# The keys of a three-layer transformer kernel projected once instead of twice, with 28 dense chunks spread over 32 scan units

## The chip, the cores and the metric

The kernel runs on one core of a Trainium2 chip as a single program. The metric is the device time of one execution in microseconds; shown is the median of the runs. The profile comes from one further execution.

## The reference

The input is `x` of 512 tokens by 1024 features, in float32. It passes through two layers of a first block, and through one layer of a second block.

```
for l in range(2):                                  # first block
    h = rms_norm(x); proj = h @ w_in[l]             # sb_q, sb_k, sb_v, sw_q (8 heads), sw_k, sw_v (2 heads), gates
    y_sb  = stick_breaking_attention(sb_q, sb_k, sb_v) @ w_branch_sb
    q, k  = rope(rms_norm per head(sw_q)), rope(rms_norm per head(sw_k))   # heads of 64
    y_swa = sliding_window_sink_attention(q, k, sw_v) @ w_branch_swa
    x = x + (sigmoid(gates) * (y_sb, y_swa) summed) @ w_out
    x = x + square(relu(rms_norm(x) @ w_up)) @ w_down
h = rms_norm(x) * (1 + scale) + shift               # second block
z, xbc, dt, q, kc, vc, ks, vs, kw, vw, gates... = h @ w_in_2     # q: 16 heads; each key and value: 2 heads of 64
y_ssm = mamba2(z, conv(xbc), dt)                    # chunked scan: 4 chunks of 128 tokens, 32 heads
y_nsa = attention over compressed, selected and windowed keys kc, ks, kw (rotated) and values vc, vs, vw
x = x + gate * (merged @ w_o); x = x + gate2 * mixture_of_experts(x); out = rms_norm(x)
```

Eight query heads share two key heads in the sliding window attention (four each), and sixteen share two in the second block. So a key head has 64 rows, and 128 rows hold both.

## The kernel before, in words

**Layout.** Activations lie feature-major: 128 partitions hold 128 features, 512 columns are the tokens. A key head of 64 features fills one half of the partitions. A matmul of a query head with a key head wants both in the same half. The even query heads are in the lower half, the odd ones in the upper half, so each of the two key heads is wanted in both halves. The kernel gets this by projecting each key head twice: `twice` loads the 64 weight columns of a head into two places of the weight tile, so that one chunk of 128 output rows holds the same head in both halves.

**Weight tiles.** Weights come in tiles of 1024 rows by 256 columns (1 MB). SyncE issues four loads into `raw[q]` (`W.issue`, L169), as soon as that place's last tile has been split. ScalarE writes a rounded part `hi` (`split_hi`, L176, 1.9 us), VectorE the rest `lo` (`split_lo`, L181, 2.3 us). A place `q` of 0 or 1 is split again when the tile in it is done. A tile gives two chunks (`dense(2t)` and `dense(2t+1)`) of 128 output rows. A chunk is 8 k-steps of three matmuls of 128 x 512 (`products`, L199 to L201): 24 matmuls.

**`mix` (first block, once per layer).** TensorE, ScalarE, VectorE and SyncE each run a queue written out by hand. Tiles 0 to 17 are: 0 the keys, 1 and 2 the window's queries, 3 the window's values, 4 and 5 values, 6 to 9 queries and keys, 10 to 17 gates. Chunks of tiles 0 to 7 alternate between PSUM banks 0 and 1; from tile 8 on (`ONE_BANK`) all are written to bank 0, so each waits for the eviction (L855) of the one before. The keys need: the two chunks of tile 0, `square` of each, `head_sums` (L562) of each, the mean, root and reciprocal (`mean_of`, `root_of`, `scale_by`) of each, and a rotation (`rotate`, L583, and `rope`, L887 to L893) of each. The queries need `query_sums` (L568), `query_mean` and four rotations. Rotations follow chunks 10 to 15, the keys' last. Then `band_scores(0)` (L593) starts the window's attention.

The first eviction needs the token factor `x_rs`, whose mean, root and reciprocal are made on VectorE and ScalarE at the beginning of `mix`.

**The scan (`ssd`, second block).** The state-space scan runs in 32 units (8 groups of 4 heads, 4 chunks of tokens). TensorE's queue is, for each unit n: `front(n+1)`, in odd units a `step` (L1665 to L1667), `dense(n+2)`, `back(n)` (L1696, L1698, L1702). The dense chunks are the projections of z (16 chunks), q (8) and the keys and values of the second block (8: kc, vc, ks and kw, two chunks each, by `twice`). ScalarE and VectorE follow with `exps` and `segment`, `weigh`, `finish`. `back(n)` waits for `weigh(n)`. Each chunk is evicted by ScalarE (L1734) into a stage of four, from where GpSimd's queue sends it to HBM (`spilled`, 128 rows by 512). Behind every second chunk the next tile but one is split.

```
for n in range(N):
    if n + 1 < N:
        front(n + 1)
    if n in due:
        step(due[n])
    if n + 2 < N:
        dense(n + 2)
    back(n)
```

**Behind the scan.** `ssm_out` loads six key chunks back (L1940) and eight query chunks (L1942) from HBM, rotates the keys late in the stage (L1969), and issues the weights of the next gates behind these loads on SyncE's queue. `nsa_project` loads the two value chunks `vc`.

Of the kernel before, what the change touches and what calls it, by code (L numbers as in the profile page):

```python
# [344 lines left out]
class FirstBlock(Kernel):  # L345
# [5 lines left out]
    def layer_tile(self, l, m, q):  # L351
# [4 lines left out]
        if t == T_SWK:  # L356
            return self.twice(w_in, C_SWK)
# [20 lines left out]

    def twice(self, w, at):

        out = []
        for j in range(2):
            src = w[:, at + j * HD:at + (j + 1) * HD].rearrange("(k p) n -> p k n", p=P)
            for r in range(2):
                a = (2 * j + r) * HD
                out.append((lambda t, a=a: t[:, :, a:a + HD], src))
        return out
# [48 lines left out]
    def mix(self):  # L436
        nc, W, l, base = self.nc, self.W, self.l, self.base
        BAND = 2 * P
        heads, chunks = 6, 2
        order = (4, 5, 0, 1, 2, 3)  # L440
        turns = [(b, j) for b in range(TB) for j in range(2) if b > 0 or j == 0]
        with ExitStack() as st:
# [5 lines left out]
                "squared", "summed", "mean", "root", "inverse", "normed", "turned_q", "cosd", "sind", "roped", "scaled"))  # L448
            s_ready, s_taken, maxed, negd, expd, sunk, added, inv_ready, p_ready, turned, t_taken, ow_ready, ow_taken = (sem(x) for x in (
# [41 lines left out]
            def kept(t, c):  # L491
                if t == T_SWK:
                    return x[:, 4 + c, :]
# [26 lines left out]
            turning = (2, 3, 4, 5, 0, 1)  # L520
# [8 lines left out]
            def _(pe):  # L529
                def dense(i, ks=range(KC)):  # L530
                    t, c = divmod(i, 2)
                    m, q = base + t // 2, t % 2
                    if ks[0] == 0:
                        if c == 0:
                            pe.wait_ge(W.lo_ready, 2 * m + q + 1)
                        if t >= 1 and (c == 1 or t >= ONE_BANK):
                            W.read(pe, base + (t - 1) // 2, (t - 1) % 2)
                        if c == 0 and t >= 1:
                            pe.wait_ge(taken0, t)
                        if c == 1 and t >= ONE_BANK:  # L540
                            pe.wait_ge(taken0, t + 1)
                    out, cols = bank(t, c), slice(c * P, (c + 1) * P)
                    if t == T_SWV and c == 1:
                        pe.wait_ge(taken0, t + 1)
# [12 lines left out]
                    if ks[-1] == KC - 1:  # L557
                        mm.then_inc(half if c == 0 else W.tile_done, 1)
# [5 lines left out]
                def query_sums(i):  # L564
                    pe.wait_ge(squared, i + 1)
                    pe.wait_ge(x_mean, 2)
                    c = order[i]
# [9 lines left out]
                def rotate(i):  # L577
                    if i < 2:
                        pe.wait_ge(normed, i + 1)
                    else:  # L580
                        pe.wait_ge(scaled, 1)
                        pe.wait_ge(q_mean, 1)
                    pe.matmul(self.ps[:, 2 + i, :], self.c("rot") if i < 2 else rot_q[:], x[:, order[i], :], start=True, stop=True).then_inc(turned_q, 1)  # L583
# [117 lines left out]
            def _(act):  # L701
                def dense(i):
# [5 lines left out]
                    elif T_SBV <= t < T_SBQ:  # L708
                        if c == 0:
                            act.wait_ge(half, t + 1)  # L710
# [10 lines left out]
                def square(i):  # L721
                    if i >= 2:
                        act.wait_ge(summed, i - 1)
                    t = T_SWK if i < 2 else T_SWQ + i // 2 - 1
                    if i % 2 == 0:
                        act.wait_ge(taken0, t + 1)
# [59 lines left out]
                dense(0)  # L786
                dense(1)
                square(0)
                square(1)
                for i in range(2, 6):  # L790
                    dense(i)
                square(2)
                square(3)
                root_of(0)
                root_of(1)
                dense(6)
                square(4)
                square(5)
                dense(7)
                dense(8)  # L800
                act.wait_ge(summed, 6)
# [39 lines left out]
            def _(dve):  # L841
                def dense(i):
                    t, c = divmod(i, 2)
                    m, q = base + t // 2, t % 2
                    if not T_SBV <= t < T_SBQ and i != 2 * T_SWV + 1:
                        if c == 0:
                            dve.wait_ge(half, t + 1)
# [7 lines left out]
                        dve.scalar_tensor_tensor(kept(t, c), bank(t, c), factor, x_rs[:], ALU.mult, ALU.mult).then_inc(taken0 if c == 0 else W.evicted[q], 1)  # L855
# [2872 lines left out]
```

## Time and profile before

| | |
|---|---|
| median of 3 runs | 2810.71 us (2810.57 to 2812.26) |
| profiled execution, its own time | 2810.99 us |
| its span in the profile | 2809.2 us, so 1.8 us lie around it |
| mean granted clock of TensorE | 0.962 |
| layer 0's `mix` starts on TensorE | 32.5 us |
| layer 1's `mix` starts | 773.9 us |
| the scan's units | from 1687 to 1962 us |

Times in the rows below are microseconds from the span's start; PE is TensorE, PEld its weight loads, DVE VectorE, ACT ScalarE, POOL GpSimd and SP SyncE. `[x <-y]` at the end of a row of the timeline is the idle time of the engine ahead of it and what released it. PEclk is the granted clock of TensorE: 1.00 is 2.4 GHz and 0.50 is 1.2 GHz. L855 is line 855 of the kernel before.

### The profile page before, as it was taken

How to read it: one execution, taken by the hardware profiler on the slowest of the kernel's cores; microseconds unless marked ns; L12 is line 12 of the kernel's file. 1: busy time of each engine (PE TensorE's matmuls, PEld its weight loads, DVE VectorE, ACT ScalarE, POOL GpSimd, SP SyncE). 2: the span in 40 equal slices, each digit the busy share in tenths (PEclk: the TensorE clock that was granted, in tenths of full speed). 3: DMA queues.
4: the chain of work that ended last, by engine and by line, in shares of the span. 5: the costliest groups of instructions: out<-in, count | busy, mean ns of one | idle time of the engine just before them, and what ended most of it. 6: DMA issues, size and time to landing. Idle time of an engine off the chain costs nothing. (4 is left out here: it accounts for less than half of the span.)

```text
span 2809.2 us, 34558 instructions
## 1 busy us (share of the span) xinstructions
PE 2639.8 (94%) x14085; PEld 2074.4 (74%) x14085; DVE 1529.0 (54%) x2173; ACT 983.2 (35%) x1359; POOL 333.5 (12%) x193
## 2 busy tenths in 40 slices
PE   8999999999999999999998999999999798989984
PEld 6877788888787777888886887887777565775542
DVE  4664555554547445644665644665764787364313
ACT  3246532322323464422232322333531487320001
POOL 0000003442200000422440000000000000011110
PEclk9999999999999999999999989999999898989997
DMA  4211143444322112443442322343343001258995
GB/s 137 91 61 60 60 135 106 136 136 135 98 76 75 61 46 90 135 135 106 134 135 75 91 80 90 101 98 97 126 146 117 16 1 76 92 211 360 418 420 238
DMA packets 274791, 351.25 MB, mean 125 GB/s; under 512 B 55108, under 2 KB 251972, under 8 KB 261956
## 3 DMA queue, kind: packets, MB, share of 16 engines
q1 hardware_dynamic: 266084, 327.97, 34.7%
q0 software_dynamic: 8448, 20.98, 2.0%
q8 instruction: 114, 1.87, 0.3%
q14 instruction: 49, 0.40, 0.0%
q10 hardware_dynamic: 96, 0.02, 0.0%
HBM read 332.13 MB, written 25.17 MB: 127 GB/s over the span
## 5 line engine op out<-in xcount | busy, mean ns | idle before, releaser
L199 PE MATMUL ps<-h_hi,w_hi 128*128 128x512 f32 x1776 | 713.8, 402 | 23.5 <-DVE h_lo L319 7.5
L200 PE MATMUL ps<-h_lo,w_hi 128*128 128x512 f32 x1776 | 697.7, 393 | 0.0
L201 PE MATMUL ps<-h_hi,w_lo 128*128 128x512 f32 x1776 | 697.4, 393 | 0.0
L176 ACT ACTIVATE w_hi<-w_raw 128x2048 fp32r<-128x2048 f32 (+1 forms) x170 | 322.2, 1896 | 793.9 <-PE ps L201 771.3
L181 DVE TENSOR_TENSOR w_lo<-w_raw,w_hi 128x2048 fp32r<-128x2048 f32 (+1 forms) x170 | 434.3, 2555 | 237.4 <-ACT w_hi L176 237.4
L199 PEld LDWEIGHTS ps<-h_hi,w_hi 128*128 128x128 f32 x1776 | 337.6, 190 | 106.5 <-issue 38.0
L200 PEld LDWEIGHTS ps<-h_lo,w_hi 128*128 128x128 f32 x1776 | 337.9, 190 | 71.2 <-issue 4.1
L201 PEld LDWEIGHTS ps<-h_hi,w_lo 128*128 128x128 f32 x1776 | 337.0, 190 | 72.0
L201 PE MATMUL ps<-merged_hi,w_lo 128*128 128x512 f32 x640 | 252.8, 395 | 0.0
L199 PE MATMUL ps<-merged_hi,w_hi 128*128 128x512 f32 x640 | 252.8, 395 | 0.0
L200 PE MATMUL ps<-merged_lo,w_hi 128*128 128x512 f32 x640 | 252.8, 395 | 0.0
L1261 POOL TENSOR_TENSOR room<-room,silu_c 128x2048 f32<-128x2048 f32 x24 | 99.5, 4147 | 1192.9 <-DMA room<-in_w_ada 1192.9
L1207 DVE TENSOR_TENSOR x<-x,ps 128x1024 f32<-128x1024 f32 x40 | 48.9, 1222 | 238.8 <-PE ps L201 238.8
L200 PEld LDWEIGHTS ps<-merged_lo,w_hi 128*128 128x128 f32 x640 | 120.1, 188 | 29.2
L201 PEld LDWEIGHTS ps<-merged_hi,w_lo 128*128 128x128 f32 x640 | 120.1, 188 | 29.1
L199 PEld LDWEIGHTS ps<-merged_hi,w_hi 128*128 128x128 f32 x640 | 120.1, 188 | 29.1
L1264 POOL TENSOR_TENSOR room<-room 128x1024 f32<-128x1024 f32 (+1 forms) x48 | 140.4, 2925 | 3.8
L855 DVE SCALAR_TENSOR_TENSOR room<-ps,x_rs 128x512 f32<-128x512 f32 x60 | 41.4, 691 | 142.2 <-PE ps L201 142.2
L1225 DVE TENSOR_TENSOR merged_lo<-room,merged_hi 128x1024 fp32r<-128x1024 f32 x32 | 99.0, 3094 | 0.0
L3202 ACT ACTIVATE moe_silu<-ps 128x256 f32<-128x256 f32 x16 | 6.1, 383 | 221.5 <-PE ps L3132 221.5
L2650 ACT ACTIVATE nsa_p<-nsa_p,nsa_mx 128x512 f32<-128x512 f32 (+3 forms) x128 | 70.8, 554 | 18.6 <-DVE nsa_mx L2601 17.0
L1221 DVE SCALAR_TENSOR_TENSOR room<-ps,room 128x1024 f32<-128x1024 f32 x32 | 39.1, 1223 | 64.7 <-PE ps L201 64.5
(482 smaller groups left out, 3736.1 us busy)
## 6 DMA issues: line engine op xcount, KB each, us to landing
w_raw<-in_w_in SPq DMA_DIRECT2D x284, 256.0 KB, 3.7
w_raw<-in_w_up SPq DMA_DIRECT2D x128, 256.0 KB, 3.6
w_raw<-in_w_down SPq DMA_DIRECT2D x128, 256.0 KB, 3.6
room<-in_w_ada SPq DMA_DIRECT2D x96, 256.0 KB, 5.9
expert_over_h<-in_w_exp_down SPq DMA_DIRECT2D x10, 1024.0 KB
w_raw<-in_w_out SPq DMA_DIRECT2D x32, 256.0 KB, 3.4
spilled<-projected POOLq DMA_DIRECT2D x32, 256.0 KB, 2.3
w_raw<-in_w_ssm_out SPq DMA_DIRECT2D x32, 256.0 KB, 3.6
```

The source lines that it names most:

```text
L176: act.activation(self.hi[:, q, :, 0:cols], raw[:, q, :, 0:cols], ACT.Copy).then_inc(self.hi_ready, 1)
L181: dve.tensor_tensor(self.lo[:, q, :, 0:cols], raw[:, q, :, 0:cols], self.hi[:, q, :, 0:cols].bitcast(F32), ALU.subtract).then_inc(self.lo_ ...
L199: pe.matmul(out, w[0], x[0], start=start, stop=False)
L200: pe.matmul(out, w[0], x[1], start=False, stop=False)
L201: return pe.matmul(out, w[1], x[0], start=False, stop=stop)
L855: dve.scalar_tensor_tensor(kept(t, c), bank(t, c), factor, x_rs[:], ALU.mult, ALU.mult).then_inc(taken0 if c == 0 else W.evicted[q], 1)
L1207: dve.tensor_tensor(two(self.x, t), two(self.x, t), self.pst[:, q, 0:n, :], ALU.add).then_inc(W.evicted[q], 1)
L1221: dve.scalar_tensor_tensor(r[:, q], self.pst[:, q, 0:n, :], 0.0, rs.unsqueeze(1).to_broadcast([P, n, S]), ALU.max, ALU.mult).then_inc(W.ev ...
L1225: dve.tensor_tensor(two(u[1], t), r[:, q], two(u[0], t).bitcast(F32), ALU.subtract).then_inc(u_low, 1)
L1261: pool.tensor_tensor(w, w, c, ALU.mult).then_inc(ada_step, 1)
L1264: pool.tensor_tensor(w[:, 0:half], w[:, 0:half], w[:, half:2 * half], ALU.add).then_inc(ada_step, 1)
L2650: act.activation(p[:, i, e, 0:W], p[:, i, e, 0:W], ACT.Exp, bias=mx[:, i, e:e + 1], scale=-1.0, accum_out=den[:, i, e:e + 1]).then_inc(exp ...
```

## The change

The key tile of a layer is loaded and split with 128 columns, each key head once, and projected as one chunk: head 0 in the lower half, head 1 in the upper half. Its square, head sums, mean, root, reciprocal and rotation are done once. The rotation's last add writes head 0 to `x[0:64, 4]` and head 1 to `x[64:128, 5]`, and two transfers on GpSimd's queue, from SBUF to SBUF, copy them to the other halves. `band_scores(0)` waits for these (`doubled`). Chunk 1 is gone; the chunks keep their numbers otherwise. As tile 0 has one chunk, chunk 2 writes bank 0 right behind chunk 0. The rotations stand behind chunks 10 to 14, the keys' first.

In the second block kc, vc, ks and kw are projected once: one chunk each, in two tiles instead of four, so the scan has 28 dense chunks. Their 28 x 8 = 224 k-steps are dealt out as 7 to each of the 32 units, so a chunk can end inside a unit's share. ScalarE's evictions and the splits follow in the unit in which a chunk ends. The loads of keys and values from HBM take one head (64 rows by 512) twice, once to each half of the partitions: 12 for the keys and 4 for the values.

```diff
         if t == T_SWK:
-            return self.twice(w_in, C_SWK)
+            return quarters_of(w_in[:, C_SWK:C_SWK + SWK], SWK)
...
-        heads, chunks = 6, 2
-        order = (4, 5, 0, 1, 2, 3)
+        heads = 5
+        order = (4, 0, 1, 2, 3)
...
-            turning = (2, 3, 4, 5, 0, 1)
+            turning = (0, 1, 2, 3, 4)
...
-                        if t >= 1 and (c == 1 or t >= ONE_BANK):
+                        if t >= 1 and (c == 1 or t == 1 or t >= ONE_BANK):
                             W.read(pe, base + (t - 1) // 2, (t - 1) % 2)
-                        if c == 0 and t >= 1:
-                            pe.wait_ge(taken0, t)
+                        if c == 0 and t >= 2:
+                            pe.wait_ge(taken0, t - 1)
...
                     if i == 0:
                         pe.wait_ge(roped, heads)
+                        pe.wait_ge(doubled, 32 * (l + 1))
...
-                for i in range(6):
+                dense(0)
+                for i in range(2, 6):
                     dense(i)
                 head_sums(0)
-                head_sums(1)
                 dense(6)
+                query_sums(1)
                 query_sums(2)
+                dense(7)
                 query_sums(3)
-                dense(7)
                 query_sums(4)
-                query_sums(5)
                 dense(8)
                 dense(9)
                 turn_sums()
                 for n, i in enumerate(turning):
                     dense(10 + n)
                     rotate(i)
+                dense(15)
                 dense(16)
                 band_scores(0)
...
-                    dve.tensor_tensor(x[:, c, :], tc[:, n % 2], ts[:, n % 2], ALU.add).then_inc(roped, 1)
+                    if i == 0:
+                        for r, to in ((slice(HD, P), 5), (slice(0, HD), 4)):
+                            e = dve.tensor_tensor(x[r, to, :], tc[r, n % 2], ts[r, n % 2], ALU.add)
+                        e.then_inc(roped, 1)
+                    else:
+                        dve.tensor_tensor(x[:, c, :], tc[:, n % 2], ts[:, n % 2], ALU.add).then_inc(roped, 1)
...
                 pool.sem_clear(clear)
+                pool.wait_ge(roped, 1)
+                pool.dma_start(x[HD:P, 4, :], x[0:HD, 4, :]).then_inc(doubled, 16)
+                pool.dma_start(x[0:HD, 5, :], x[HD:P, 5, :]).then_inc(doubled, 16)
+                pool.wait_ge(doubled, 32 * (l + 1))
...
-P_XBC, P_SMALL, P_Z, P_Q, P_KK, P_GS, P_SSMO, P_GA, P_NSAO, P_WO, P_MOE = 0, 6, 7, 11, 13, 15, 17, 21, 23, 25, 27
+P_XBC, P_SMALL, P_Z, P_Q, P_KK, P_GS, P_SSMO, P_GA, P_NSAO, P_WO, P_MOE = 0, 6, 7, 11, 13, 14, 16, 20, 22, 24, 26
+KEYS_FROM = ((24, 0), (24, 1), (26, 0), (26, 1), (27, 0), (27, 1))
+VALUES_FROM = 25
...
-            return self.twice(w_in, (C_KC, C_VC, C_KS, C_KW)[t - 2 * P_KK])
+            return both(C_KC, NKV, C_VC, NKV) if q == 0 else both(C_KS, NKV, C_KW, NKV)
...
+        CHUNKS = 4 * (P_GS - P_Z)
+        PARTS = CHUNKS * KC // N
...
+            ended = [[i for i in range(CHUNKS) if (KC * i + KC - 1) // PARTS == n] for n in range(N)]
...
+                def dense(n):
+                    for part in range(PARTS * n, PARTS * (n + 1)):
+                        i, k = divmod(part, KC)
+                        (m, q), c = pair_of(i), i % 2
+                        if k == 0:
+                            start(i)
+                        cols = slice(c * P, (c + 1) * P)
                         mm = products(pe, dense_ps(i), (W.hi[:, q, k, cols], W.lo[:, q, k, cols]), (self.h[0][:, k, :], self.h[1][:, k, :]), k == 0, k == KC - 1)
+                        if k == KC - 1:
+                            mm.then_inc(half if c == 0 else W.tile_done, 1)
...
+                def denses(n):
+                    for i in ended[n]:
+                        dense(i)
...
                 for i in range(6):
-                    sp.dma_start(self.rp[:, 8 + i, :], self.spilled(self.key_chunk(i))).then_inc(k_landed[i], 16)
+                    for r in range(2):
+                        sp.dma_start(self.rp[r * HD:(r + 1) * HD, 8 + i, :], self.spilled_heads(*KEYS_FROM[i])).then_inc(k_landed[i], 16)
```

## Rows read from the trace of the kernel before

**Rows 1.** The page: busy time of each engine, share of the span, instructions.
```profile
PE 2639.8 (94%) x14085; PEld 2074.4 (74%) x14085; DVE 1529.0 (54%) x2173; ACT 983.2 (35%) x1359; POOL 333.5 (12%) x193
```

**Rows 2.** Windows: length, busy by engine (instructions), PEclk, DMA share, GB/s.
```profile
126.00:128.00 2.00, 2.00 (x9) 1.28 (x8) 0.69 (x2) 1.98 (x2) 0.00 (x0) 1.00 0.00 0
...
1711.00:1781.00 70.00, 69.92 (x410) 57.42 (x411) 38.55 (x86) 21.41 (x36) 4.86 (x9) 1.00 0.33 109
...
1957.00:1962.00 5.00, 3.71 (x32) 3.28 (x32) 2.99 (x9) 0.07 (x2) 0.00 (x0) 0.50 0.51 159
```

**Rows 3.** Waits of TensorE, 1687 to 1962: total, times, longest.
```profile
PE ps L1696 <- DVE ssd_l L1811: 5.1, 1, 5.1
```

**Rows 4.** Timeline, layer 0's start: start, duration, instruction, idle before.
```profile
32.48 0.47 PE L199 MATMUL ps<-h_hi,w_hi 128*128 128x512 f32 x1 [0.32 <-PEq L1418]
...
34.39 3.35 DVE L933 RECIPROCAL x_rs<-x_rs 128x512 f32<-128x512 f32 x1 [1.15 <-ACT x_rs L782]
...
37.77 0.39 PE L201 MATMUL ps<-h_hi,w_lo 128*128 128x512 f32 x1
...
38.28 0.69 DVE L855 SCALAR_TENSOR_TENSOR room<-ps,x_rs 128x512 f32<-128x512 f32 x1 [0.50 <-PE ps L201]
```

**Rows 5.** Timeline, 60 to 78, the end of tile 2.
```profile
65.20 1.88 PE L562 MATMUL ps<-mix_room_w,const_first 128*128 128x512 f32 x4
...
66.52 0.79 PE L199 MATMUL ps<-h_hi,w_hi 128*128 128x512 f32 x1
...
67.15 0.40 PE L200 MATMUL ps<-h_lo,w_hi 128*128 128x512 f32 x1
```

**Rows 6.** Timeline, around layer 0's last rotation.
```profile
125.50 1.02 PE L583 MATMUL ps<-room,const 128*128 128x512 f32 x2
...
126.49 0.47 PE L199 MATMUL ps<-h_hi,w_hi 128*128 128x512 f32 x1
...
126.80 0.39 PE L200 MATMUL ps<-h_lo,w_hi 128*128 128x512 f32 x1
```

**Rows 7.** Timeline, a scan unit behind a tile's end.
```profile
1783.38 0.39 PE L201 MATMUL ps<-h_hi,w_lo 128*128 128x512 f32 x1
...
1786.12 0.48 PE L199 MATMUL ps<-h_hi,w_hi 128*128 128x512 f32 x1
...
1790.08 0.68 DVE L1815 TENSOR_TENSOR ssd_e<-ssd_e,bc 128x512 f32<-128x512 f32 x1
...
1791.78 0.45 PE L1696 MATMUL ps<-ssd_l,x_dt 128*64 128x128 f32 x4
```

**Rows 8.** Timeline, a scan unit with a step (L1665, L1787).
```profile
1794.29 0.60 PE L1665 MATMUL ps<-const,xs 128*128 128x128 f32 x4
...
1794.97 0.48 PE L199 MATMUL ps<-h_hi,w_hi 128*128 128x512 f32 x1
...
1795.53 0.68 DVE L1787 TENSOR_TENSOR x_dt<-ps,dt 128x512 f32<-128x512 f32 x1
...
1796.92 0.69 DVE L1811 TENSOR_TENSOR ssd_l<-ssd_l,c_b 128x512 f32<-128x512 f32 x1
```

**Rows 9.** Timeline, start of the kernel.
```profile
12.16 5.89 PE L1449 MATMUL ps<-const,x_tokens 128*128 128x128 f32 x28
...
14.63 1.91 ACT L176 ACTIVATE w_hi<-w_raw 128x2048 fp32r<-128x2048 f32 x1 [7.90 <-DMA w_raw<-in_w_in]
...
17.89 1.02 PE L1460 MATMUL ps<-squares,const 128*128 128x512 f32 x2
```

**Rows 10.** SyncE's queue, 1960 to 2180.
```profile
2069.64 4.43 SPq L1940 DMA_DIRECT2D nsa_q_k<-spilled  x6
...
2078.18 25.22 SPq L169 DMA_DIRECT2D w_raw<-in_w_in  x12
```

**Rows 11.** Tile nsa_q_k, 1960 to 2150: duration min/median/max, first and last start.
```profile
L1969 PE MATMUL ps<-nsa_q_k,const x12: 590/592/594, 2084.1 to 2100.0; 128*128 128x512 f32 x12
...
DMA to landing us min/median/max: 5.2/6.4/7.7
```

More of the change, by code:

```diff
@@ L557, in dense @@
                     if ks[-1] == KC - 1:
-                        mm.then_inc(half if c == 0 else W.tile_done, 1)
+                        mm.then_inc(half if c == 0 and t != T_SWK else W.tile_done, 1)
                 def head_sums(i):
@@ L577, in rotate @@
                 def rotate(i):
-                    if i < 2:
-                        pe.wait_ge(normed, i + 1)
+                    if i == 0:
+                        pe.wait_ge(normed, 1)
                     else:
                         pe.wait_ge(scaled, 1)
-                        pe.wait_ge(q_mean, 1)
-                    pe.matmul(self.ps[:, 2 + i, :], self.c("rot") if i < 2 else rot_q[:], x[:, order[i], :], start=True, stop=True).then_inc(turned_q, 1)
+                    pe.matmul(self.ps[:, 2 + i, :], self.c("rot") if i == 0 else rot_q[:], x[:, order[i], :], start=True, stop=True).then_inc(turned_q, 1)
                 def band_scores(i):
@@ L845, in dense @@
                     if not T_SBV <= t < T_SBQ and i != 2 * T_SWV + 1:
-                        if c == 0:
-                            dve.wait_ge(half, t + 1)
+                        if c == 0 and t != T_SWK:
+                            dve.wait_ge(half, t)
                         else:
@@ L854, in dense @@
                         factor = HD ** -0.5 if T_SBQ <= t < T_SBK else 1.0
-                        dve.scalar_tensor_tensor(kept(t, c), bank(t, c), factor, x_rs[:], ALU.mult, ALU.mult).then_inc(taken0 if c == 0 else W.evicted[q], 1)
-                    if c == 1 and t + 1 < tiles:
+                        dve.scalar_tensor_tensor(kept(t, c), bank(t, c), factor, x_rs[:], ALU.mult, ALU.mult).then_inc(taken0 if c == 0 and t != T_SWK else W.evicted[q], 1)
+                    if (c == 1 or t == T_SWK) and t + 1 < tiles:
                         W.split_lo(dve, m + 1, q, cols=width(t + 2))
@@ L934, in _ @@
                 dve.wait_ge(x_ready, 2)
-                for i in range(6):
+                dense(0)
+                for i in range(2, 6):
                     dense(i)
                 mean_of(0)
-                mean_of(1)
                 dense(6)
@@ L948, in _ @@
                 rope(1)
-                for n in range(2, 6):
+                for n in range(2, 5):
                     dense(10 + n)
                     rope(n)
+                dense(15)
                 dense(16)
@@ L1021, in tail @@
             two = lambda a, t: a[:, n * t:n * t + n, :]
+            next_width = lambda j, t: SWK if not last and j + 1 == QUARTERS and t == 2 else COL
             @block.sync
@@ L1645, in _, with start @@
             def _(pe):
-                def dense(i):
+                def start(i):
                     (m, q), c = pair_of(i), i % 2
@@ L1653, in dense @@
                         W.read(pe, *pair_of(i - 2))
-                    cols = slice(c * P, (c + 1) * P)
-                    for k in range(KC):
+                def dense(n):
[5 more added lines that the diff above has]
+                        cols = slice(c * P, (c + 1) * P)
                         mm = products(pe, dense_ps(i), (W.hi[:, q, k, cols], W.lo[:, q, k, cols]), (self.h[0][:, k, :], self.h[1][:, k, :]), k == 0, k == KC - 1)
-                    mm.then_inc(half if c == 0 else W.tile_done, 1)
+                        if k == KC - 1:
+                            mm.then_inc(half if c == 0 else W.tile_done, 1)
                 def step(G):
@@ L1760, in _ @@
                 step(0)
-                dense(0)
+                denses(0)
                 act.wait_ge(ac_ready, 1)
@@ L1768, in _ @@
                 exps(0)
-                dense(1)
+                denses(1)
                 for n in range(N):
@@ L1775, in _ @@
                     if n + 2 < N:
-                        dense(n + 2)
+                        denses(n + 2)
             @block.vector
@@ L1873, in _ @@
                 pool.sem_clear(clear)
-                for i in range(N):
+                for i in range(CHUNKS):
                     if i % 2 == 0:
@@ L2203, in _ @@
                 for c in range(NG):
-                    sp.dma_start(self.vc[:, c, :], self.spilled(26 + c)).then_inc(v_landed, 16)
+                    for r in range(2):
+                        sp.dma_start(self.vc[r * HD:(r + 1) * HD, c, :], self.spilled_heads(VALUES_FROM, c)).then_inc(v_landed, 16)
                 for x in range(4):
```

74 lines of the change are left out of this document (33 added, 41 removed).

## Prediction

> **What bounds the kernel now.** I read the page's busy shares first: TensorE is busy for 94% of the span [rows 1], so a microsecond taken off its work counts unless a wait takes its place. The profile's chain of waits is no use here: it covers almost none of the span. So I went to the waits of TensorE and to windows over the two places where the change acts. In the scan, 70 us in its middle have TensorE busy for 69.92 us, VectorE for 38.55 and ScalarE for 21.41 [rows 2]; over the whole scan TensorE waits on VectorE once for long, 5.1 us [rows 3]. Both places are bound by TensorE's queue. A busy matmul overlaps its neighbour, so its price is its spacing, not its duration: in layer 0 the matmuls of six dense chunks (6 x 24 = 144) run from 32.48 to 65.20 [rows 4, 5], 0.227 us each, 5.45 us a chunk. The 0.39 us that each row shows as duration would overprice the change by 70%.
>
> **The layers' keys, twice (layer 0 and 1).** Chunk 1 of the key tile goes: -5.45. One of the two `head_sums` goes: two of them, started at 65.20, put the second matmul of the next chunk at 67.15 where it would have been at 65.43, 1.72 us for two [rows 5]: -0.86. One rotation goes as well, but it is the last one, behind chunk 15. From chunk 16 on all chunks write bank 0 and wait for the eviction before; with the rotation in between, the next chunk starts 0.99 us after the last one's end, at 126.49, and its second matmul comes at 126.80, 0.31 later [rows 6]. That is the eviction's time (0.2 us of signal, 0.69 of work), so the rotation only fills a wait: 0, at most -0.86.
>
> New: chunk 0 and chunk 2 now follow each other in bank 0, with no chunk in bank 1 between. The last matmul of chunk 0 starts at 37.77 and the next would at 38.00; the eviction starts at 38.28 and takes 0.69 [rows 4], so chunk 2 starts near 39.07, and loses 0.08 more on its first spacing as in [rows 6]: +1.15. The factor it needs (the reciprocal, 34.39 plus 3.35) is there before, at 37.74 [rows 4]; were it later, the wait would be longer, so the bounds are 1.0 and 2. Tile 2's halves, the next thing due, are split behind chunk 0 in some 5 us, under the 10.9 us of tile 1.
>
> Each layer: 5.45 + 0.86 - 1.15 = 5.16; both: -10.3 (bounds -8.6 and -12.0).
>
> At nothing: the narrower split of the key tile (it lies under the last down tile, or under the transposes at the start), the second half-height add in the keys' rotation (0.7 us more on VectorE, in a stretch of 5.45 us chunks with an eviction of 0.69 each, and one whole rotation less behind it), and the two transfers on GpSimd's queue. They start when the first rotated key is there, near 107, and `band_scores(0)` waits for them behind chunks 12 to 16, five chunks or 27 us later; the longest landing that I find for a 256 KB move is 7.7 us [rows 11]. If that cover were gone, the 7.7 us would stand ahead of the scores, and the softmax, the turns and all later chunks are behind them. GpSimd has nothing else queued in this stage.
>
> **The scan.** Four of 32 chunks go: 4 x 5.45 = -21.8. The other 28 are cut into 32 pieces of seven eighths. The number of switches between dense and scan matmuls stays at 32, so their cost stays. What must be asked is whether the shorter cover uncovers the chain behind a tile's end: ScalarE's eviction, its split, VectorE's split, `segment`, and the `weigh` that `back` waits for. Before: the tile's last matmul starts at 1783.38 and ends 0.39 later, 1783.77; the last `weigh` ends at 1790.76; `back` starts at 1791.78 [rows 7]. The chain is 7.0 long and TensorE gives it 8.0. After, a tile's end falls 1 to 7 parts deep in a piece of 7 (a part is 3 matmuls, 0.68 us). At 7 of 7 (units 15 and 31) TensorE gives 8.0 - 0.68 = 7.3 against 7.0: 0.3 left. At 6 of 7 in unit 22 a step follows: it adds 1.39 on VectorE (1795.53 to 1796.92) and 0.68 on TensorE (1794.29 to 1794.97) [rows 8], so 8.7 against 8.4: again 0.3. All other ends have more. So no new wait, but thin. In throughput VectorE needs 38.55 of 70 us [rows 2], and 10% less TensorE time leaves it far from full. The 5.1 us wait at the end [rows 3] stays, since tile 13 still ends with the last piece. Bounds for the scan: -21.8 and, if the chain decided every unit, 0.
>
> **Behind the scan.** Key loads become 12 of half height instead of 6, two more for the values. Six issues took 4.43 us [rows 10], so six more cost SyncE about 4.4: the gate weights are issued near 2082.6 instead of 2078.18 [rows 10], for a tile that TensorE reaches only after its rotations, the last of which runs at 2100.0 [rows 11]. The first keys, issued at 2069.64 with 6.4 us to landing, are there at 2076 or 2077 against a first rotation at 2084.1 [rows 10, 11]: hidden, with 7 us left.
>
> **Sum.** -10.3 - 21.8 = -32.1 on the profiled execution's 2810.99 gives 2778.9. The median, 2810.71, is 0.3 below it; 2779 for both.
>
> **Rivals.** *The scan's chain decides.* If the chain is 1 us longer than I read it, the 14 tile ends stall by some 0.7 us each, 10 us: 2789; if it decided every unit the scan would save nothing, 2801. For it: the 0.3 us left. Against it: only the ends in units 15 and 22 are that tight (the one in 31 has its wait already). *The new wait costs the clock.* TensorE's granted clock is 0.50 (1.2 of 2.4 GHz) in the 5 us behind the scan's 5.1 us wait [rows 2, 3]. If the new 1.15 us did that, each layer would lose half of 5 us or more: 2 x 2.5 = 5, 2784. Against it: after the 0.99 us pause of [rows 6] the granted clock is 1.00 [rows 2]. The Trainium skill, page "TensorE: Matmul & The Clock Gate", section "A second HAM failure mode: psum-queue depth-cycling", says that small pauses between groups of matmuls can make the clock oscillate; this trace does not show it at pauses of 1 us, and by that rule it would be 2784 or above. *The start gets shorter.* ScalarE waits 7.90 us for the first key tile, until 14.63 [rows 9]; its load halves. But TensorE transposes without a break from 12.16 to 18.05 and its sums start at 17.89 [rows 9], so the tile isn't what is waited for: 0. If the smaller loads let the tokens land sooner, 1 to 3 us: 2776. *Slower.* ScalarE and VectorE run their queues in the written order, and a unit's exponentials now stand behind a chunk end whose place changes from unit to unit. If that left `back` waiting in each of the 32 units, the kernel would be slower from 32.1 / 32 = 1.0 us a unit; at 1.5 us, 2827. Against it: in the units with no tile end the chain has no split in it, and four units have no chunk end at all.
>
> **Chances.** As forecast 0.78 (own range 2774 to 2786); the chain 0.10; the clock 0.05; the start 0.04; slower 0.03. The predicted time is the likeliest's. The range 2773 to 2791 holds the clock, the start and the mild form of the chain, and leaves out about 0.1. A measurement of this kernel can tell about 0.2%, 5.6 us: faster by more 0.96, within it 0.01, slower 0.03.
>
> **What the profile after would show.** Right: 144 fewer dense matmuls; one wait of about 1 us of chunk 2 on L855's successor in each layer, at granted clock 1.00; the scan 21 to 22 us shorter with one long wait at its end; each layer's mixing about 5 us shorter; the rotations of the second block's keys waiting for nothing. Wrong: waits of `back` on `weigh` in units 15, 22 or in many; a longer wait of `band_scores(0)`; a granted clock of 0.50 behind chunk 0; a span that shrinks by much more than 32 us would mean that the stages' starts hung on something that I took as hidden.

## The result and the profile after

| kernel | us, median (lowest to highest, runs) | before, same chip | ratio to before (95%) |
|---|---|---|---|
| the change | 2777.61 (2776.12 to 2782.88, 4) | 2811.19 | 0.9882 (0.9867 to 0.9897) |
| the change, once more (experiment 9) | 2779.17 (2774.28 to 2784.64, 5) | 2810.03 | 0.9894 (0.9879 to 0.9909) |
| before, once more (experiment 10) | 2808.03 (2803.74 to 2814.37, 12) | 2810.03 | 0.9991 (0.9982 to 1.0001) |

The change makes the kernel 1.1 to 1.2% faster: 33.6 us in the first comparison, 30.9 in the second. The intervals leave some 4 us on either side of each. The forecast was -32.1, 2779. The profiled execution took 2776.12 us, 34.9 less than that of before. The page, span and TensorE's line (busy us, share, instructions):

```profile
span 2774.0 us, 34212 instructions
...
PE 2599.5 (94%) x13933; PEld 2042.5 (74%) x13933; DVE 1513.6 (55%) x2159; ACT 972.9 (35%) x1349; POOL 334.6 (12%) x193
```

TensorE is 40 us less busy than in [rows 1] and has 152 products less: the 144 dense ones of six chunks, and 8 of the sums and rotations. The new wait in layer 0 is there, and no other near it. The timeline, from the last matmul of chunk 0 over its eviction to the first two of chunk 2, and the window behind it (length, busy times, granted clock third from the end):

```profile
38.12 0.39 PE L201 MATMUL ps<-h_hi,w_lo 128*128 128x512 f32 x1
...
38.63 0.69 DVE L844 SCALAR_TENSOR_TENSOR room<-ps,x_rs 128x512 f32<-128x512 f32 x1 [0.54 <-PE ps L201]
...
39.47 0.47 PE L199 MATMUL ps<-h_hi,w_hi 128*128 128x512 f32 x1 [0.96 <-DVE room L844]
...
39.77 0.39 PE L200 MATMUL ps<-h_lo,w_hi 128*128 128x512 f32 x1
```

```profile
40.00:44.00 4.00, 4.00 (x19) 3.29 (x18) 2.29 (x1) 1.05 (x2) 0.00 (x0) 1.00 0.02 3
```

From 38.12 to 39.77 there are two spacings, 1.65 us where two of 0.227 are the norm: 1.20 us lost, and the granted clock is 1.00 behind it. Where the last rotation stood [rows 6], there is now a wait:

```profile
121.77 0.47 PE L199 MATMUL ps<-h_hi,w_hi 128*128 128x512 f32 x1 [0.83 <-issue]
```

It starts 88.98 us into the stage, where before it was 126.49 - 32.48 = 94.01: 5.03 us less, against 5.16 in the sum. TensorE's waits in the scan (total, times, longest):

```profile
PE ps L1712 <- DVE ssd_l L1831: 5.0, 1, 5.0
PE ps L1681 <- DVE x_dt L1807: 1.7, 1, 1.7
```

These are the waits of before, the long one at the end among them [rows 3]; there is no wait in a unit. The tile end that falls 7 of 7 parts deep lies in the piece of unit 15, which TensorE works off two units ahead; its split stands before `weigh` and `back` of unit 14. On the timeline, VectorE's split, that `weigh`'s last operation, and the `back` that needs it:

```profile
1804.34 2.29 DVE L181 TENSOR_TENSOR w_lo<-w_raw,w_hi 128x2048 fp32r<-128x2048 f32 x1 [2.89 <-ACT w_hi L176]
...
1808.19 0.69 DVE L1835 TENSOR_TENSOR ssd_e<-ssd_e,bc 128x512 f32<-128x512 f32 x1
...
1809.21 0.20 PEld L1712 LDWEIGHTS ps<-ssd_l,x_dt 128*64 128x64 f32 x4 [0.35 <-issue]
```

The `weigh` ends at 1808.88 and `back` starts at 1809.21: 0.33 us of slack, where the prediction worked out 0.3. Behind the scan, the tile view of the second block's keys, for the rotations (count, ns, first and last start) and the transfers (us to landing), and SyncE's queue with the key loads and the next weights:

```profile
L1987 PE MATMUL ps<-nsa_q_k,const x12: 590/592/594, 2057.7 to 2073.6; 128*128 128x512 f32 x12
...
DMA to landing us min/median/max: 3.1/4.3/5.8
```

```profile
2043.14 7.51 SPq L1958 DMA_DIRECT2D nsa_q_k<-spilled  x12
...
2054.64 2.95 SPq L169 DMA_DIRECT2D w_raw<-in_w_in  x4
```

The first keys, issued from 2043.14 with at most 5.8 us to landing, are there by 2049.5, and the first rotation is at 2057.67: 8 us of cover where the prediction had 7. The last of the twelve is issued by 2050.65, and its rotation is the last of those up to 2073.6. No rotation waits for a load.

Stage by stage, though, the two profiled executions differ in a way that the sum doesn't have. The stages' starts are those matmuls in front of which TensorE waited for its sequencer; the length is the difference of two starts, in us:

| stage | before | after | difference | in the sum |
|---|---|---|---|---|
| mix, layer 0 | 280.96 | 276.79 | -4.17 | -5.16 |
| tail, layer 0 | 460.44 | 461.82 | +1.38 | 0 |
| mix, layer 1 | 282.59 | 278.81 | -3.78 | -5.16 |
| scan | 274.77 | 254.35 | -20.42 | -21.8 |
| `nsa_compress` | 43.81 | 39.41 | -4.40 | 0 |
| the other stages behind the scan | 803.27 | 799.10 | -4.17 | 0 |
| kernel's start; tail of layer 1 with the projections | 663.36 | 663.72 | +0.36 | 0 |

The touched stages gave 28.4 us, less the 1.4 lost in the tail, and stages with unchanged work gave 8.6. The sum is right to within some microseconds, and the parts seem not to be. That is what most experiments are about.

### The profile page after: what moved, and what is told of

It is laid out like the page before. It is cut to its first block and busy times, and to the rows that moved or that the text cites. A ratio compares the mean times of both kernels' runs of the same rounds, so it can differ in the third digit from the quotient of the medians.

```text
span 2774.0 us, 34212 instructions
## 1 busy us (share of the span) xinstructions
PE 2599.5 (94%) x13933; PEld 2042.5 (74%) x13933; DVE 1513.6 (55%) x2159; ACT 972.9 (35%) x1349; POOL 334.6 (12%) x193
## 5 line engine op out<-in xcount | busy, mean ns | idle before, releaser
L199 PE MATMUL ps<-h_hi,w_hi 128*128 128x512 f32 x1728 | 695.0, 402 | 25.6 <-DVE h_lo L319 7.5
L201 PE MATMUL ps<-h_hi,w_lo 128*128 128x512 f32 x1728 | 678.9, 393 | 0.0
L200 PE MATMUL ps<-h_lo,w_hi 128*128 128x512 f32 x1728 | 678.7, 393 | 0.0
L199 PEld LDWEIGHTS ps<-h_hi,w_hi 128*128 128x128 f32 x1728 | 328.6, 190 | 106.7 <-issue 40.1
L200 PEld LDWEIGHTS ps<-h_lo,w_hi 128*128 128x128 f32 x1728 | 328.7, 190 | 69.4 <-issue 4.1
L201 PEld LDWEIGHTS ps<-h_hi,w_lo 128*128 128x128 f32 x1728 | 327.5, 190 | 70.1
```

The source lines that it names most:

```text
L199: pe.matmul(out, w[0], x[0], start=start, stop=False)
L200: pe.matmul(out, w[0], x[1], start=False, stop=False)
L201: return pe.matmul(out, w[1], x[0], start=False, stop=stop)
```

## The experiments

Experiments 1 to 4, 5 to 8 and 9 to 12 form three groups. Each group shares a chip and its own runs of before (medians 2810.25, 2809.36 and 2810.03). The changed kernel itself stands beside experiments 10 to 12 only (as experiment 9); elsewhere a distance to it is one between two sets of runs, and is given by the medians and by the ratios to before.

**1 and 2. Each half alone.** The diff is the first part of the change (layers and their loads) or the second (scan, key loads).

> The layers' part of the change alone; the second block as before. The sum of the prediction: -10.3 us against before (2800.5). From the trace of the changed kernel: its two mix stages gave -4.2 and -3.8, a tail +1.4, and the stages that the change doesn't touch -8.8 in all, with a higher granted clock there. If the stages behind the scan depend on when they start (the clock's phase), the two mix stages together give -8 to -10, and the stages from the compression to the end, untouched here, move by 1 to 9 us of either sign together with their granted clock. If their gain belongs to the narrower key loads of the second block, they stay at before's times here (within 0.5 us).

> The second block's part alone (28 chunks spread over 32 units, half-height key loads); the layers as before. The sum: -21.8 us (2789). By the trace of the changed kernel the scan gives -20.4 to -21.8, with its first microseconds at half clock or not. If the -8.8 us of the stages behind the scan come with the key loads and the shorter scan, they are here too, and the total is -29 to -30 (2781); if they depend on the stages' start times alone, they come in another size, between 0 and 9 us.

Measured: the layers alone 2802.57 us, ratio 0.9976 (0.9962 to 0.9989), so -6.7 with 3 to 11 in the interval; the second block alone 2787.52, 0.9919 (0.9904 to 0.9933), -22.8 with 19 to 27. The sum's -10.3 and -21.8 both lie in these. The layers' version does not touch the compression and yet has it at 39.60 us: it does not take the half-height key loads to bring its 4 us. That rival is out.

**9 and 10. Both kernels once more, unchanged.**

> The changed kernel once more, unchanged, for its stages and its spread. Two theories of the differences in stages that the change doesn't touch (compression 43.8 against 39.4 us, attention 174.0 against 172.4, the end of the layer's tail +1.4): by the first, the clock falls and rises at places that differ from execution to execution, and these stages differ between two executions of the same kernel by up to 5 us; the scan stays within 252.5 to 254.5, layer 0's mix within 275.9 to 276.9. By the second, they belong to the code (other key loads, other start times), and every stage comes out within 0.3 us of the first execution. Ratio to before: 0.988 +- 0.0015 by both.

> The kernel before once more, unchanged. By the theory of a clock that falls and rises at other places in each execution, the compression comes out anywhere between 39.4 and 45.0 us, the first mix stage between 280.9 and 282.6; the scan stays at 274.8 to 275.5. By the theory that these stages belong to the code, compression is 43.8, mix 281.0, within 0.3 us.

The changed kernel once more does not decide between the theories: its compression (39.56), attention (172.36) and tail (461.84) came out as in its first execution, as the second theory has it, while its first mix and its scan are 0.7 us shorter. The kernel before once more does decide. Windows of `nsa_compress` (length, busy time and count of TensorE, its weight loads, VectorE, ScalarE, GpSimd; granted clock third from the end) for before, before once more, and after:

```profile
2145.81:2189.62 43.81, 42.66 (x317) 39.99 (x317) 6.11 (x8) 8.92 (x17) 1.89 (x4) 0.79 0.25 79
```

```profile
2151.50:2191.01 39.51, 39.06 (x317) 36.48 (x317) 6.17 (x8) 8.92 (x17) 1.89 (x4) 0.86 0.29 88
```

```profile
2119.44:2158.85 39.41, 38.96 (x317) 36.38 (x317) 6.11 (x8) 8.92 (x17) 1.89 (x4) 0.86 0.29 88
```

The same kernel has 43.81 us at a granted clock of 0.79, and 39.51 at 0.86. From the start of `ssm_out` to the end, before took 847.08 us and then 838.37; the changed kernel 838.51 and 837.22. The 8.6 us are not the change's. The second theory, that the stages belong to the code, is refuted. One range that went with the first theory was missed: the first mix stage took 283.52 us, where 280.9 to 282.6 was expected.

What makes the compression long can be read further than to its mean clock. Its second group of 64 products, in before, in before once more, and a window inside it in before:

```profile
2159.32 12.29 PE L2334 MATMUL ps<-nsa_gate,cmp_w 128*128 128x62 f32 x64 [0.70 <-DMA cmp_w<-in_cmp_w_v]
```

```profile
2165.70 7.31 PE L2334 MATMUL ps<-nsa_gate,cmp_w 128*128 128x62 f32 x64
```

```profile
2162.00:2172.00 10.00, 10.00 (x48) 9.90 (x48) 0.00 (x0) 0.35 (x4) 0.00 (x0) 0.50 0.16 37
```

Before's first execution comes to these products at full clock, waits 0.70 us for their weights, and then runs at half clock. In its second one the clock is at half for some microseconds at the stage's start, so TensorE comes later into the stage, finds the weights there, and runs the products at full clock. The 14 profiled executions divide in the same way: the four that wait here (0.70 to 1.40 us) take 43.8 to 45.0 us, the ten that don't take 39.3 to 40.6, and both kinds occur with the change. So the stage's length goes with the place where the clock falls, and part of the 4 us goes through a load that is late. No run holds the load apart from the clock, so how much is whose is not shown.

Nor was the tail's 1.38 the change's: the sixteen one-column products at the end of layer 0, behind a wait of 5.6 us, in before, in after, and in before once more:

```profile
771.56 2.02 PE L1113 MATMUL ps<-const,room 128*128 128x1 f32 x16
```

```profile
767.70 3.41 PE L1112 MATMUL ps<-const,room 128*128 128x1 f32 x16
```

```profile
774.39 3.41 PE L1113 MATMUL ps<-const,room 128*128 128x1 f32 x16
```

They take 2.02 us when the clock is back in time (granted clock 0.92 over them) and 3.41 when it isn't (0.50). The Trainium skill, page "TensorE: Matmul & The Clock Gate", section "What's actually happening", says that the chip judges TensorE's activity in windows that run freely and don't start with the kernel, so that the same kernel meets the change of clock at another instruction each time. The traces agree: 2.02 and 3.41 us for the same instructions.

With several executions a stage's length can be averaged. The first row of each pair holds the kernels without that part of the change, the second those with it:

| stage | profiled executions, us | mean |
|---|---|---|
| mix 0, without | 280.96, 282.56, 283.52 | 282.35 |
| mix 0, with | 276.79, 276.83, 275.94, 276.02, 276.71, 276.07 | 276.39 |
| mix 1, without | 282.59, 282.04, 283.77 | 282.80 |
| mix 1, with | 278.81, 278.75, 278.79, 278.95, 278.94, 278.83 | 278.85 |
| scan, without | 274.77, 275.47, 275.10 | 275.11 |
| scan, with | 254.35, 253.57, 252.64, 252.91, 252.90, 253.61 | 253.33 |

Scan: -21.8, as in the sum (a seventh scan with the change, 252.82 in experiment 11, would make it -21.9). The mixes: -5.96 and -3.95, together -9.9 where the sum has -10.3.

That the two layers differ is again the clock's. Take only executions of layer 0 in which no stretch of 5 us was below full clock: 280.96 us without the change, 275.94, 276.02 and 276.07 with it, a difference of 4.95. In layer 1 no execution is free of it. With the change the clock was low both in the first 5 us (0.53 to 0.57) and behind the softmax wait, in all six; the wait behind chunk 0 then comes 8.7 us into the stage instead of 6.7, and the softmax part is worth 0.8 as in layer 0: 276.0 + 2.0 + 0.8 = 278.8, which is the mean. Without the change the two layers are alike where the clock is: 282.59 us in layer 1 of before and 282.56 in layer 0 of experiment 2, both with 0.66 in the first 5 us alone. So the change gives 4.95 in layer 0 and, by this estimate, the same in layer 1.

**3 and 11. Chunk 0 in bank 1.**

```diff
-                        if t >= 1 and (c == 1 or t == 1 or t >= ONE_BANK):
+                        if t >= 1 and (c == 1 or t >= ONE_BANK):
-            bank = lambda t, c: self.ps[:, c if t < ONE_BANK else 0, :]
+            bank = lambda t, c: self.ps[:, 1 if t == T_SWK else c if t < ONE_BANK else 0, :]
```

> The changed kernel, with the key chunk of the layers written to bank 1 instead of bank 0, so that the next chunk doesn't wait for its eviction. My price of the wait was 1.15 a layer (its trace shows 0.96 and 0.95 of idle time, and some 0.25 on the next spacing). Expected: both waits gone, each mix stage 1.2 us shorter, the total -2.4 us against the changed kernel, 2775 (ratio to before 0.9873 instead of 0.9882). Rival: the stage is held by ScalarE's and VectorE's queues behind it (the splits of the next tiles), and the wait comes back at chunk 4 or 5: 0 us. A second rival: the softmax wait further down, at half clock in the changed kernel, moves by more than 1.2 us with the phase.

> The version with chunk 0 in bank 1 beside the changed kernel on the same chip. Its first run gave ratios of 0.9880 and 0.9882 for the two, with intervals of 0.0015, so the 2.4 us (0.0009) that I expect of it were not to be told from nothing. Expected: no wait behind chunk 0, mix stages 1.1 us shorter each, total 2 to 2.5 us under the changed kernel in the same call; the rival is 0.

Measured: 2774.84 and 2772.12 us, ratios 0.9880 (0.9864 to 0.9896) and 0.9873 (0.9853 to 0.9893), against 0.9882 and 0.9894 for the changed kernel. Both waits are gone. Layer 0's mix takes 275.72 and 275.58 us against a mean of 276.39, layer 1's 277.71 and 277.58 against 278.85: -0.7 and -1.2. Like with like, the clock low behind the softmax wait alone, layer 0 has 275.58 to 275.72 against 276.71 to 276.83, so -1.1 there as well. The price of the wait is confirmed in both layers. In the whole kernel's time it lies inside the intervals: beside the changed kernel on one chip the version is 7.0 us faster, where 2 to 2.5 were expected and its stages explain 1.9. Expectation 3's second rival is real too. The first products behind the softmax wait (us, last bracket the wait ahead), in after, in this version, and in the version of experiment 8, whose mix code is the same:

```profile
137.38 1.68 PE L593 MATMUL ps<-const,swa_p 128*128 128x128 f32 x7 [2.27 <-DVE swa_p L913]
```

```profile
135.38 1.17 PE L593 MATMUL ps<-const,swa_p 128*128 128x128 f32 x7 [2.27 <-DVE swa_p L913]
```

```profile
135.89 0.98 PE L593 MATMUL ps<-const,swa_p 128*128 128x128 f32 x7 [2.27 <-DVE swa_p L913]
```

The wait is 2.27 each time. The same seven products take 1.68, 1.17 or 0.98 us, by where the clock falls. In after the granted clock of the 4 us behind them is 0.64:

```profile
138.00:142.00 4.00, 4.00 (x22) 2.94 (x22) 2.08 (x1) 2.68 (x3) 0.00 (x0) 0.64 0.00 0
```

**4 and 5. What spreading the chunks is worth.** Chunks stay whole, and four units of the scan have none: in experiment 4 those shown, in experiment 5 the last four, 28 to 31.

```diff
-            ended = [[i for i in range(CHUNKS) if (KC * i + KC - 1) // PARTS == n] for n in range(N)]
+            bare = (7, 15, 23, 31)
+            places = [n for n in range(N) if n not in bare]
+            ended = [[places.index(n)] if n in places else [] for n in range(N)]
```

> The changed kernel, but the 28 chunks of the scan stay whole, one a unit, and units 7, 15, 23 and 31 have none. A unit without a chunk leaves TensorE with the four prefix products only, before a back that needs VectorE's segment and weigh behind them: 0.2 + 1.13 + 0.69 + 0.69 + 0.2 = 2.9 us of wait, and 3 more where the chunk before ended a tile (units 15 and 31), since ScalarE's eviction and split and VectorE's split stand ahead of the segment. Expected: 2.9 + 5.9 + 2.9 + about 4 at the end = 16 us longer than the changed kernel, so 2793, and up to 2797 with the clock at half behind the pauses. If there is more slack in a unit than I read (VectorE is busy for little over half of the time), 1 to 2 us a unit: 2782.

> The changed kernel with 28 whole chunks in units 0 to 27 of the scan and none in the last four. By the price of a unit without a chunk (2.9 us of wait, from durations of rows) four of them in a row cost 4 x 2.9 = 11.6, one tile end ahead of them some 3, and the 5.0 us wait that the changed kernel has at the end is inside these: about 10 us longer; with the clock at half over the four units, which doubles their 1.9 us of matmuls each, about 18: 2787 to 2796. If a bare unit costs less than a microsecond, the time stays within 4 us of the changed kernel.

Measured: 2792.26 (0.9927, 0.9911 to 0.9942) and 2795.78 us (0.9949, 0.9931 to 0.9967), 15 and 18 above the changed kernel by the medians, 13 and 19 by the ratios. TensorE's waits ahead of `back` in experiment 4, from its rows of TensorE:

```profile
1742.43 0.66 PE L1714 MATMUL ps<-ssd_l,x_dt 128*64 128x128 f32 x8 [2.45 <-DVE ssd_l L1833]
...
1810.05 0.70 PE L1714 MATMUL ps<-ssd_l,x_dt 128*64 128x128 f32 x4 [5.23 <-DVE ssd_l L1833]
...
1877.28 0.70 PE L1714 MATMUL ps<-ssd_l,x_dt 128*64 128x128 f32 x4 [2.40 <-DVE ssd_l L1833]
...
1943.13 0.70 PE L1714 MATMUL ps<-ssd_l,x_dt 128*64 128x128 f32 x4 [5.04 <-DVE ssd_l L1833]
...
1949.71 0.70 PE L1714 MATMUL ps<-ssd_l,x_dt 128*64 128x128 f32 x4 [2.57 <-DVE ssd_l L1833]
```

The missing chunks of units 7, 15 and 23 cost 2.45, 5.23 and 2.40 us (they are missed two units ahead, in front of `back` of units 5, 13 and 21) against 2.9, 5.9 and 2.9 worked out, the end 5.04 and 2.57. That is 12.7 us more than in the changed kernel; the scan is 21.4 longer than its mean, 274.71, at a granted clock of 0.94 instead of 0.98. So the other 8.7 us go with the lower clock behind the pauses (that execution was the slowest of six; the medians differ by 15). In it four chunks less give a scan that is no shorter than before (275.11), the bound of 0 that the prediction kept. By its median the version is 18 us under before, 9.9 of them the layers', so there the scan still saves some 8. In experiment 5 the waits at the end are 5.04, 2.33, 2.57, 2.57 and 2.57 us, 10.0 more than in the changed kernel where about 10 was expected, and the scan takes 270.20 at a granted clock of 0.94. In the changed kernel no unit is bare.

**6. The doubling transfers without cover.**

```diff
                 pool.wait_ge(roped, 1)
+                pool.wait_ge(taken0, ONE_BANK)
```

> The changed kernel, with the two transfers that double the layers' rotated key issued only when chunk 16 has been evicted, so that nothing covers them. The prediction priced this cover: band_scores(0) would stand for up to 7.7 us a layer. Expected: TensorE waits 6 to 8 us less the 0.9 us that the eviction's signal takes, and then at half clock for some us: 7 to 10 us a layer, 14 to 20 in all, 2791 to 2797. Rival: the wait is absorbed by the softmax wait that follows (2.3 us in the changed kernel) and costs a third less: 10 us in all.

Measured: 2786.64 us, 0.9921 (0.9895 to 0.9948), 9 above the changed kernel by the medians and 11 by the ratios. Its mix stages take 282.74 and 284.74, so 6.3 and 5.9 over the means, 12.2 together. The first scores and the first turn behind them:

```profile
131.76 3.79 PE L584 MATMUL ps<-room 64*128 64x256 f32 x16 [4.92 <-DMA room<-room]
...
143.51 0.98 PE L593 MATMUL ps<-const,swa_p 128*128 128x128 f32 x7 [1.72 <-DVE swa_p L913]
```

A wait of 4.92 us appears (4.50 in layer 1), while the softmax wait shrinks from 2.27 to 1.72. So the cover matters as claimed, and the size, 9 to 12 us, lies by the rival's 10 and under the 14 to 20. The prediction had the landing at 7.7 us, the longest among the second block's key and query loads, issued one behind the other [rows 11]; here the two transfers land in 2.7 and 2.9 us. That they are half as large need not be the reason: the 256 KB moves of GpSimd's queue landed in 2.3 us (median) in the scan of before. From the transfers in the changed kernel, between 95 and 125 us (issues, KB each, median us to landing):

```profile
room<-room POOLq DMA_DIRECT2D x2, 128.0 KB, 3.1
```

**7. Two microseconds more work.** Nine more products ahead of the last gate tile behind the scan.

> The changed kernel with nine more matmuls of 128x512 ahead of the last gate tile behind the scan, 9 x 0.227 = 2.0 us of work whose result is overwritten. Nothing else is changed. If the stages behind have fixed durations, their rows stay and the total is +2.0 (2779.7). If what they cost hangs on when they start against the clock's changes, single stages (compression above all: 43.8 us before, 39.4 after) move by up to 4 us of either sign with their granted clock, and the total is anywhere from -3 to +7 of the changed kernel.

Measured: 2778.31 us (2767.58 to 2785.82, 4 runs), 0.9881 (0.9847 to 0.9916). `ssm_out`, with the extra 2.0 us in it, took 149.19 us, less than the 151.63 without; `nsa_compress` took 44.15. It fits, but alone it would not have told a shift's effect from chance; experiments 9 and 10 do.

**8 and 12. The end of the scan.** On top of experiment 3:

```diff
-                    if n + 2 < N:
+                    if n + 2 < N - 1:
                         dense(n + 2)
+                    elif n + 2 == N - 1:
+                        dense(N - 1, 0, 4)
+                    elif n == N - 2:
+                        dense(N - 1, 4)
                     back(n)
```

and ScalarE's eviction and split of the last tile stand behind the last exponentials, VectorE's split behind the last `weigh`.

> The version with chunk 0 in bank 1, and the end of the scan changed: the last unit's piece of a chunk is cut in two (4 and 3 parts), the second half stands behind the last prefix products, and the last tile's eviction and splits stand behind the last exponentials and the last weigh. Aimed at the 5.0 us wait at the end of the scan, which the change left as it was (VectorE's split of 2.3 us stands ahead of the last segment). From the rows of the changed kernel: the last back starts at about 28 where it started at 32 (us past 1900), the scan is 3 to 4 us shorter, 0.5 to 1 more with fewer microseconds at half clock: 2771 against 2774.8 for bank 1 alone. Rival: the split, now last, holds the next stage's first tile, and nothing is won.

> The version with chunk 0 in bank 1 and the cut end of the scan, beside the others on the same chip. Its first run had the scan at 250.7 us against 252.6 with chunk 0 in bank 1 alone, and a wait of 4.0 us at the next stage's start in place of the 5.0 us one: 1.9 us won of the 3 to 4 expected. Expected now: 1.5 to 2.5 us under the version with bank 1 alone, 3.5 to 5 under the changed kernel. Rival: the spread of the clock's phases hides it.

Measured: 2774.93 and 2771.85 us, 0.9874 (0.9852 to 0.9896) and 0.9867 (0.9850 to 0.9883). Of experiment 8, the last `back` but one, the split behind it, and the next stage's first product:

```profile
1920.69 0.45 PE L1712 MATMUL ps<-ssd_l,x_dt 128*64 128x128 f32 x4 [0.47 <-issue]
...
1922.75 2.29 DVE L181 TENSOR_TENSOR w_lo<-w_raw,w_hi 128x2048 fp32r<-128x2048 f32 x1 [0.55 <-ACT w_hi L176]
```

```profile
1927.57 0.77 PE L199 MATMUL ps<-h_hi,w_hi 128*128 128x512 f32 x1 [4.04 <-PEq L1617]
```

The 5.0 us wait is down to 0.47, with 0.60 more in front of the last `back` (1922.41). But the rival took most of it: the split now runs from 1922.75 to 1925.04, VectorE's last additions stand behind it, and the next stage's first product waits 4.04 us instead of 1.1. The scan is 250.73 us against 252.64 with bank 1 alone, 1.9 less where 3 to 4 were expected, and 250.29 against 252.82 in the second pair, 2.5 less. Against bank 1 alone on the same chip the whole time moved by -0.3 us where 1.5 to 2.5 were expected; in the first pair, on two chips, it is +0.1 by the medians and -1.7 by the ratios. None of this can be told from nothing. It is still the version with the lowest median that was run, 7.3 us under the changed kernel beside it, with intervals that barely overlap; the mechanisms account for 1.9 + 1.9 of these.

## Why the prediction was right

**The sum.** -32.1 forecast, -33.6 and -30.9 measured. The totals alone would bear any sum from -26 to -37, the outer ends of their two intervals. It is the stages that confirm the terms: the scan -21.8 (forecast -21.8), the layers -9.9 (-10.3). Layer 0's mean of -5.96 and layer 1's of -3.95 miss 5.16 in opposite directions and that by the clock; with the clock's part taken out it is 4.95. The -34.9 of the two executions that were profiled first is no better confirmation, since 8.6 of it came from stages that the change doesn't touch.

**The layers.** TensorE reached the chunk behind the old rotation 5.03 us earlier (5.16). The new wait cost 1.20 (1.15). The rotation's price of nothing held: its place is now an idle 0.83 us. In the changed kernel's layer 0, 0.9 us was given back behind the softmax wait (from 137.38 to the products of L618 at 205.07 it is 67.69 us, and 66.77 in experiment 4 with the same code), and in layer 1 the first 5 us ran at a granted clock of 0.56, where before had 0.66. Neither has to come with the edit: before once more has 0.50 there, and experiment 8, with the layers' change and chunk 0 in bank 1, has 0.66 and full clock behind the softmax wait, and takes 276.37 us.

**The scan.** The slack of 0.3 us in unit 15 was measured at 0.33. In unit 22 it is 1.2 (the second `weigh` ends at 1862.87, `back` starts at 1864.05), and the prediction had 0.3. It had taken the step at 1.39 us of VectorE from a unit further ahead; the step in unit 22 belongs to the last chunk of tokens, which keeps no state, so that VectorE's trace has only one operation of 0.68 there.

**What was hidden.** Loads, transfers and splits cost nothing, as forecast, with two prices too high. The doubling transfers land in 3.1 us, not 7.7. The twelve key loads take 7.5 us of SyncE's queue, 3.1 more than the 4.43 of the six [rows 10], and not 4.4 more.

**The rivals.** The chain did not decide; it does when a unit is left bare (experiments 4 and 5). The new wait did not cost the clock behind it. The prediction's reason for this was misread, though: the 0.99 us of [rows 6] is no pause, as the rotation fills it (125.50 to 126.52). The trace of before has real ones, waits of 0.85 to 0.96 us for evictions in layer 0's mix, with the clock full throughout. But the same trace also has a short pause with a fall of the clock behind it: in the compression the granted clock is 0.50 from 2161.2 on, 1.9 us behind the end of the 0.70 us wait. Whether a shorter start exists can't be said: the kernel's start took 31.2 to 33.1 us over all executions, with and without the change.

**What was not foreseen.** The prediction read two executions' difference as the change's: "each layer's mixing about 5 us shorter" was 4.2 and 3.8 in the pair shown and 6.0 and 3.9 in the means, and "a span that shrinks by much more than 32 us would mean that the stages' starts hung on something" would have misled, had the span come out a few us lower. Its bound of 5.6 us for a measurement was fair for medians, but a single profiled stage carries up to 5 us of the clock's chance.

## What to carry to other kernels

Compare stages over several executions before explaining one: a stage that the change doesn't touch, or the same kernel profiled twice, shows how much of a difference is the clock's. Then look for a wait that only the long executions have. When work is taken out of a stage where one engine covers another's chain, spread what is left evenly: a whole piece of 5.45 us that was missing in one unit cost 2.4 to 5.2 us of waiting there, and a lower clock behind it. A wait at the end of a queue is seldom removed by moving the work that causes it past the last consumer: ask who stands behind it in its new place.

## What the runs showed of the hardware

- The same program, on the same chip, took 2801.17 to 2815.20 us in 17 runs (before, beside experiments 1 to 4), with mean granted clocks of 0.960 to 0.970 and a correlation of -0.80 between the two. Single stages vary by more of their length: compression 39.3 to 45.0 us, attention 172.2 to 176.2, over 14 profiled executions of kernels in which neither was changed.
- A pause of 2.27 us ahead of seven 128x128 products left them at full speed (0.98 us) or at 1.68; pauses of 0.83 to 0.96 us in layer 0's mix of before and of the changed kernel were followed by a granted clock of 1.00.
- In the compression a wait of 0.70 to 1.40 us for weights was followed by half clock, and a stage of 43.8 to 45.0 us, in four executions of four. In the ten without this wait the same products ran at full clock, and the stage took 39.3 to 40.6.
- Transfers of 128 KB from one half of SBUF's partitions to the other, issued by GpSimd, landed in a median of 3.1 us in layer 0 of the changed kernel, where three weight loads of 256 KB were in flight as the first one was issued, and in 2.7 and 2.9 us in layer 0 of experiment 6.
